# The delta rule's triangular inverse on 32x32 array tiles for four of six levels, and the sample tokens' products 128 wide

## The reference

```
a_mat = I + strict_lower(beta * decay * (k k^T))
sol   = solve_triangular(a_mat, [beta*v | beta*exp(gamma)*k])   # unit lower
w = u - wk @ S ;  o = qg @ S + (q k^T * decay) @ w ;  S = g_last*S + kd^T w
```

## Time and profile before

| | us |
|---|---|
| median of 3 runs (lowest, highest) | 2129.26 (2129.2, 2131.8) |
| the profiled execution: its time | 2131.32 |
| its span, first to last instruction | 2129.6 |
| TensorE busy | 2109.6 (99%) |
| VectorE busy | 1212.0 (57%) |
| ScalarE busy | 778.5 (37%) |
| GpSimd busy | 183.5 (9%) |
| mean granted TensorE clock | 0.996 of full speed |

### The profile page before, as it was taken

How to read it: one execution, slowest core, us unless ns; L and a number is a source line. 1 busy time by engine, 2 the same in 40 slices (tenths; PEclk the granted TensorE clock), 3 DMA queues, 4 the chain that set the end, 5 groups by cost and what they waited for, 6 DMA issues and landing times.

```text
span 2129.6 us, 34124 instructions
## 1 busy us (share of the span) xinstructions
PE 2109.6 (99%) x14525; PEld 2073.3 (97%) x14525; DVE 1212.0 (57%) x1978; ACT 778.5 (37%) x976; POOL 183.5 (9%) x347
## 2 busy tenths in 40 slices
PE   9999999999999999999999999999999999999997
PEld 9999999999999999999999999999999999999997
DVE  7988787555576566655545454444444444444444
ACT  6434554233223223334333443333333333333333
POOL 7000011110132110110000000000000000000001
PEclk9999999999999999999999999999999999999998
DMA  7544453444543444465544444444444444444443
GB/s 233 147 140 131 143 166 110 120 130 121 159 142 107 120 130 121 139 194 152 150 149 149 149 149 150 150 150 153 150 149 149 149 150 150 152 150 151 149 149 109
DMA packets 295638, 309.40 MB, mean 145 GB/s; under 512 B 9712, under 2 KB 290416, under 8 KB 295232
## 3 DMA queue, kind: packets, MB, share of 16 engines
q1 hardware_dynamic: 291616, 291.54, 44.9%
q0 software_dynamic: 3584, 15.55, 2.5%
q10 hardware_dynamic: 288, 0.15, 0.0%
HBM read 298.83 MB, written 8.37 MB: 144 GB/s over the span
## 4 chain that ended last, share of the span: by engine, by line
PE 88%; DVE 8%; ACT 2%; issue 1%; DMA 1%; SPq 0%; DVEq 0%; ACTq 0%
PE main L1494 27%; PE main L1495 27%; PE main L1496 27%; PE aux L1616 6%; DVE scratch L926 2%; DVE lo L919 2%; DVE scratch L919 1%; DMA raw<-in_w_in 1%; DVE scratch L923 1%; ACT hi L645 0%; PE aux L1726 0%; DVE qkv L926 0%; PE aux L1601 0%; ACT scratch L673 0%; SPq L241 0%
## 5 line engine op out<-in xcount | busy, mean ns | idle before, releaser
L919 DVE TENSOR_TENSOR lo<-raw,hi 128x1024 fp32r<-128x1024 f32 x546 | 660.1, 1227 | 350.9 <-ACT hi L645 343.9
L1494 PE MATMUL main<-x_hi,hi 128*128 128x320 f32 x2688 | 841.3, 313 | 4.7 <-DVE lo L919 2.3
L1496 PE MATMUL main<-x_hi,lo 128*128 128x320 f32 x2688 | 831.2, 309 | 0.0
L1495 PE MATMUL main<-x_lo,hi 128*128 128x320 f32 x2688 | 831.1, 309 | 0.0
L645 ACT ACTIVATE hi<-raw 128x1024 fp32r<-128x1024 f32 x546 | 567.3, 1054 | 696.7 <-DMA raw<-in_w_up 201.7
L1494 PEld LDWEIGHTS main<-x_hi,hi 128*128 128x128 f32 x2688 | 505.5, 188 | 12.1 <-DVE lo L919 7.4
L1495 PEld LDWEIGHTS main<-x_lo,hi 128*128 128x128 f32 x2688 | 505.6, 188 | 0.8
L1496 PEld LDWEIGHTS main<-x_hi,lo 128*128 128x128 f32 x2688 | 505.2, 188 | 0.0
L1494 PE MATMUL main<-o_hi,hi 128*128 128x320 f32 x1408 | 441.3, 313 | 0.0
L1496 PE MATMUL main<-o_hi,lo 128*128 128x320 f32 x1408 | 435.0, 309 | 0.0
L1495 PE MATMUL main<-o_lo,hi 128*128 128x320 f32 x1408 | 435.0, 309 | 0.0
(11 more groups left out here) (272 smaller groups left out, 1200.8 us busy)
## 6 DMA issues: line engine op xcount, KB each, us to landing
raw<-in_w_in SPq DMA_DIRECT2D x210, 512.0 KB, 3.6
raw<-in_w_up SPq DMA_DIRECT2D x128, 512.0 KB, 3.7
raw<-in_w_down SPq DMA_DIRECT2D x128, 512.0 KB, 3.5
raw<-in_w_back SPq DMA_DIRECT2D x80, 512.0 KB, 3.5
scratch<-in_s_in POOLq DMA_DIRECT2D x8, 512.0 KB, 4.8
out_s_out<-scratch POOLq DMA_DIRECT2D x8, 512.0 KB, 4.4
merged<-in_x SPq DMA_DIRECT2D x8, 320.0 KB, 7.7
qkv<-in_x POOLq DMA_DIRECT2D x1, 2560.0 KB, 11.2
```

Of the source, the lines that this page charges most:

```text
L919: return dve.tensor_tensor(out, a, b, op)
L1494: pe.matmul(bank, hi, xh, start=first, stop=False)
L1495: pe.matmul(bank, hi, xl, start=False, stop=False)
L1496: return pe.matmul(bank, lo, xh, start=False, stop=last)
```

## The change

The three units' 32x32 diagonal blocks are kept beside each other in compact tiles (`XTC`, `XXC`, `YYC`, 32 columns for each unit), and the first four levels (blocks up to 32) work on 32x32 tiles of the array: tile (i, i) holds the i-th diagonal block. TensorE computes Y and then (X Y)^T only; X is turned out of X^T by DVE's 32x32 transposes. At the end of level 3 (for the samples, level 1) DVE writes the blocks back to the diagonals of the full `XT` and `XX`, which POOL has cleared. TensorE's and DVE's step 2 goes. The samples' operands are read 128 columns wide: k k^T and q k^T are one product, and no product of steps 1 to 15 has a 64-column stationary operand. The wait for `tok_scaled` moves from step 4 to step 11. A new semaphore `x_cleared` holds TensorE's step 1. POOL folds the masks to 32 columns (`CM`) before the first `history`.

```diff
-            for level in range(2, 6): level_mask(level)
-            select(M1T[:], ...) x3
+            select(FM[:, 0:P], ...) x3
+            ch.link(pool.tensor_copy(FM[:, 5 * P:6 * P], ident[:]))
+            fm = FM.rearrange("p (m j c) -> p m j c", m=6, j=4)
+            ch.link(pool.tensor_tensor(fm[:, :, 0:2, :], fm[:, :, 0:2, :], fm[:, :, 2:4, :], ALU.add))
+            ch.link(pool.tensor_tensor(CM.rearrange("p (m c) -> p m c", m=6), fm[:, :, 0, :], fm[:, :, 1, :], ALU.add))
...
                 pool.dma_start(A["p_out"][h], S1).then_inc(ss_stored, 16)
+                if following:
+                    pool.memset(XT[:, 0:NP], 0.0)
+                    pool.memset(XX[:, 0:NP], 0.0).then_inc(x_cleared, 1)
...
 DVE, step 1
+                    tt(LT[:, 0:NP], AX[0][:, 0:NP], DTM[:, 0:NP], ALU.mult)
+                    link(tt(LT[0:NS, NP:N], AX[1][0:NS, N:N + NS], DTM[0:NS, NP:N], ALU.mult))
+                    for i in range(4):
+                        ins = tt(blocks(YYC, i), diagonal(LT, i), mask(0, i), ALU.mult)
+                    link(ins)
+                    tt(XTC[:, 0:2 * CB]..., mask(5), YYC[:, 0:2 * CB]..., ALU.subtract)
+                    link(tt(XTC[0:NS, 2 * CB:3 * CB], CM[0:NS, 5 * CB:6 * CB], YYC[0:NS, 2 * CB:3 * CB], ALU.subtract))
+                    dve.transpose(XXC[:, 0:2 * CB], XTC[:, 0:2 * CB])
+                    dve.transpose(XXC[0:NS, 2 * CB:3 * CB], XTC[0:NS, 2 * CB:3 * CB]).then_inc(x_ready, 1)
 DVE, even steps of levels 0 to 2 (samples: levels 0 and 1)
+                        ins = tt(XTC[:, 0:2 * CB], XTC[:, 0:2 * CB], AX[0][:, P:P + 2 * CB], ALU.subtract)
+                        link(ins)
+                        ins = dve.transpose(XXC[:, 0:2 * CB], XTC[:, 0:2 * CB])
 DVE, even step of level 3
+                        for i in range(4):
+                            r = slice(CB * i, CB * (i + 1))
+                            ins = tt(diagonal(XT, i, 2), XTC[r, 0:2 * CB]..., AX[0][r, P:P + 2 * CB]..., ALU.subtract)
+                        link(ins)
+                        for i in range(4):
+                            ins = dve.transpose(diagonal(XX, i, 2), diagonal(XT, i, 2))
...
 TensorE
-                elif k == 2:
-                    (transposes of XT, three products)
+            def tiles32(level):
+                for u in range(3 if level < 2 else 2):
+                    for i in range(4 if u < 2 else 2):
+                        yield (u, i, slice(CB * i, CB * (i + 1)), slice(CB * u, CB * (u + 1)),
+                               slice(u * P + CB * i, u * P + CB * (i + 1)))
 step 1
-                    for n, lo, hi in units:
-                        mm(AX[0][0:n, lo:hi], KT[:, lo:hi], KB[:, lo:hi])
-                        mm(AX[1][0:n, lo:hi], KT[:, lo:hi], QT[:, lo:hi])
+                    for lo in (0, P):
+                        mm(AX[0][:, lo:lo + P], KT[:, lo:lo + P], KB[:, lo:lo + P])
+                        mm(AX[1][:, lo:lo + P], KT[:, lo:lo + P], QT[:, lo:lo + P])
+                    mm(AX[1][:, NP:NP + P].rearrange("p (g n) -> p g n", g=2), wide_k[:, NP:NP + P], QKS)
 odd steps, even steps of levels 0 to 3
+                        for u, i, r, c, at in tiles32(level):
+                            ins = mm(AX[0][r, c], LT[r, at], XXC[r, c])
+                        for u, i, r, c, at in tiles32(level):
+                            ins = mm(AX[0][r, P + CB * u:P + CB * (u + 1)], YYC[r, c], XTC[r, c])
```

More of the change, by code:

```diff
@@ L31 @@
 CT = 32
+CB, SMALL_LEVELS = 32, 4
 C_MIX, C_MLP, C_FIN, C_CW = 0, KD, 2 * KD, 3 * KD
@@ L370, in level_mask @@
                 s = 2 << level
-                m = LM[:, level * P:(level + 1) * P]
+                m = FM[:, (level + 1) * P:(level + 2) * P] if level < SMALL_LEVELS else \
+                    LM[:, (level - SMALL_LEVELS) * P:(level - SMALL_LEVELS + 1) * P]
                 nb = P // (2 * s)
@@ L625, in dn_steps @@
             steps = {}
-            for k in range(19):
+            for k in (0, 1, *range(3, 19)):
                 pos = dn_place(k, False)[0] + 4
@@ L1207, in merge, with beside, diagonal, blocks @@
                     .then_inc(mlo_ready, 1)
-            both = ((P, slice(0, NP), True), (NS, slice(NP, N), False))
+            both = ((P, slice(0, NP)), (NS, slice(NP, N)))
+            def beside(t, i, j):
+                return t[CB * i:CB * (i + 1), 0:NP].rearrange("p (u x) -> p u x", u=2)[:, :, CB * j:CB * (j + 1)]
+            def diagonal(t, i, units=None):
+                if units == 2 or i >= 2:
+                    return beside(t, i, i)
+                tail = t[CB * i:CB * (i + 1), CB * i:CB * i + 2 * P + CB]
+                return bass.AP(tail.tensor, tail.offset, [list(tail.ap[0]), [P, 3], [1, CB]])
+            def blocks(t, i):
+                n = 3 if i < 2 else 2
+                return t[CB * i:CB * (i + 1), 0:n * CB].rearrange("p (u c) -> p u c", u=n)
+            def mask(m, i=None):
+                if i is None:
+                    return CM[:, None, m * CB:(m + 1) * CB].to_broadcast([P, 2, CB])
+                return CM[CB * i:CB * (i + 1), None, m * CB:(m + 1) * CB].to_broadcast([CB, 3 if i < 2 else 2, CB])
             def dn_step(h, k):
@@ L1255, in dn_step @@
                     dve.wait_ge(z_psum, h * 6 + (level + 1))
[L1256 to L1261, removed]
+                    if level < SMALL_LEVELS - 1:
+                        ins = tt(XTC[:, 0:2 * CB], XTC[:, 0:2 * CB], AX[0][:, P:P + 2 * CB], ALU.subtract)
+                        c = slice(2 * CB, 3 * CB)
+                        if level == 0:
+                            ins = tt(XTC[0:NS, c], XTC[0:NS, c], AX[0][0:NS, P + 2 * CB:P + 3 * CB], ALU.subtract)
+                        if level == 1:
+                            for i in range(2):
+                                r = slice(CB * i, CB * (i + 1))
+                                ins = tt(XT[r, NP + CB * i:NP + CB * (i + 1)], XTC[r, c], AX[0][r, P + 2 * CB:P + 3 * CB],
+                                         ALU.subtract)
+                        link(ins)
+                        ins = dve.transpose(XXC[:, 0:2 * CB], XTC[:, 0:2 * CB])
+                        if level == 0:
+                            ins = dve.transpose(XXC[0:NS, c], XTC[0:NS, c])
+                        ins.then_inc(x_ready, 1)
+                    elif level == SMALL_LEVELS - 1:
+                        for i in range(4):
+                            r = slice(CB * i, CB * (i + 1))
+                            ins = tt(diagonal(XT, i, 2), XTC[r, 0:2 * CB].rearrange("p (u c) -> p u c", u=2),
+                                     AX[0][r, P:P + 2 * CB].rearrange("p (u c) -> p u c", u=2), ALU.subtract)
+                        link(ins)
+                        for i in range(4):
+                            ins = dve.transpose(diagonal(XX, i, 2), diagonal(XT, i, 2))
+                        ins.then_inc(x_ready, 1)
+                    else:
+                        if level < 5:
+                            tt(XX[:, 0:NP], XX[:, 0:NP], AX[2][:, 0:NP], ALU.subtract)
+                        ins = tt(XT[:, 0:NP], XT[:, 0:NP], AX[3][:, 0:NP], ALU.subtract)
+                        ins.then_inc(x_ready, 1)
                 elif k == 16:
@@ L1646, in dn_step @@
                     pe.wait_ge(x_ready, h * 7 + (level + 1))
-                    for n, lo, hi in units[:3 if level < 2 else 2]:
-                        ins = mm(AX[1][0:n, lo:hi], LT[:, lo:hi], XX[:, lo:hi])
+                    if level < SMALL_LEVELS:
+                        for u, i, r, c, at in tiles32(level):
+                            ins = mm(AX[0][r, c], LT[r, at], XXC[r, c])
+                    else:
+                        if level == SMALL_LEVELS:
+                            pe.wait_ge(tok_scaled, h + 1)
+                        for lo in (0, P):
+                            ins = mm(AX[1][:, lo:lo + P], LT[:, lo:lo + P], XX[:, lo:lo + P])
                     ins.then_inc(y_psum, 1)
@@ L1652, in dn_step @@
                     pe.wait_ge(y_ready, h * 6 + (level + 1))
[L1653 to L1658, removed]
+                    if level < SMALL_LEVELS:
+                        for u, i, r, c, at in tiles32(level):
+                            ins = mm(AX[0][r, P + CB * u:P + CB * (u + 1)], YYC[r, c], XTC[r, c])
+                    else:
+                        for lo in (0, P):
+                            if level < 5:
+                                mm(AX[2][:, lo:lo + P], XT[:, lo:lo + P], YY[:, lo:lo + P])
+                            ins = mm(AX[3][:, lo:lo + P], YY[:, lo:lo + P], XT[:, lo:lo + P])
                     ins.then_inc(z_psum, 1)
```

82 lines of the change are left out of this document (38 added, 44 removed).

## The result

The median fell from 2129.23 us (2128.95 to 2131.8, 4 runs) to 2095.03 us (2094.36 to 2095.44, 4 runs): ratio 0.9835, 95% interval 0.9823 to 0.9848. The profiled execution's span is 2093.6 us, 36.0 less than that of before.

A forecast was written before the change was run, and what follows sets the result against it. TensorE's stream was taken as the bound: -18.6 us from its steps, -1.7 and +0.2 from waits in heads, +0.2 and +1.6 from POOL make -18.3, so the median 2129.3 becomes 2111.0 us. Range 2100 to 2126.

The forecast's parts named there:

- What bounds the kernel: TensorE's stream, busy 99% of the span: a microsecond taken out of it anywhere is a microsecond off the end.
- What is there today: Gaps that delta-rule steps 1 to 15 cost TensorE before the change, read from its timeline: 11.64 us per head.
- The round trip: TensorE going to another tile shape and back, charged 0.35 us once for every new step on small tiles.
- The price of an instruction on a small tile: Each 32x32 TensorE instruction in levels 0 to 3 was taken to cost 25 ns, with 18 and 37 ns as ends.
- The first rival: Instructions on small tiles overlap more than forecast: at 18 ns each the time would be 2103 us; chance 0.20.
- the loads' 18 ns: Pace of step 16's weight loads on 128x32 tiles in the earlier trace, used as a low price per small instruction.
- DVE's waits: TensorE's waits for DVE inside a head: 1.7 us less for six heads and 0.2 us more at step 10.
- The wait of step 5: TensorE's 0.28 us wait for DVE between steps 4 and 5 in regular heads goes: -1.7 us for six heads.
- Step 10: DVE's longest new step, with four transposes: 1.25 us, late by 0.1 us in the two peeled heads, +0.2 us in all.
- the prediction's own sign: The forecast was to count as wrong if TensorE waits for DVE's turned tiles in each head.
- POOL at the start: POOL's 2.1 us of mask folding ahead of the first history, less 0.5 slack, costs TensorE 1.6 us; bounds 0 and 2.5.
- The rival on PSUM: Four row tiles writing one PSUM bank take turns: 56 ns per small instruction, 2147 us; chance 0.08.

## Why the prediction was right in sign and wrong in size

- **What bounds the kernel: right.** TensorE's stream set the end, and the sum of the gaps' changes less the waits gives the span's change to 0.1 us.
- **What is there today: right.** The gaps of before needed no correction, and the 128-wide steps came out as charged, 1.77 for 1.79 and 1.12 for 1.12; alone they gave 5.7 us by the medians where the gaps say 5.1.
- **The round trip: right.** Charged 0.35 us, the line's fixed part is 0.335. The Trainium skill ("TensorEngine Tiling (Array Packing)", Key Properties) says that a change of tiling mode drains the array, and gives no price. The traces have the price; no run here shows that a drain is its cause.
- **The price of an instruction on a small tile: the step that failed.** The prediction had it as "I take 25 ns: the same quarter-wide columns, the same pair of loads and passes on one tile after another." It read the distance between starts in the earlier trace rows as what an instruction costs. It was the load of four busy tiles, 4 x 0.107 us over 16 instructions, and so it goes with the columns streamed: 64 columns gave 1.00 us in place of 1.22, and 32 columns give 0.030 us per instruction on the busiest tile. A small step has 4 to 6 on its busiest tile, 0.12 to 0.18 us, and was charged 0.40 to 0.50. Per head the eight small steps were charged 6.40 us and took 3.86, 20.3 us in all. The first rival named the mechanism, and then priced it by the loads' 18 ns, which was no price of a 32-column product either. With the 0.107 us that it used, which no row of before has but which the durations of 273 and 219 ns bear out, 32/128 x 0.107 is 0.027 us for an instruction on a tile, and that arithmetic was there to be done.
- **DVE's waits: one right, one missed.** The wait of step 5 went as forecast. Step 10 was charged 1.25 us and took 1.92: an operation on 32 partitions and 64 columns took 0.23 us (four subtractions in 0.91) or 0.245 (four transposes in 0.98), where an overlapped one was charged 0.13. The wait comes in all eight heads, 3.8 us where 0.2 was charged. By the prediction's own sign, TensorE waiting for DVE's turned tiles in each head, this term was wrong too. Step 18 of head 4 adds 0.6 us that was not charged.
- **POOL at the start: right in kind.** Charged 1.6 us. The wait near 54 us grew by 1.4, as forecast, but all waits of the first 60 us only by 0.8, and moving the fold gave 1.1 by the medians, within their noise.
- **The sum**: the 18.3 us forecast, 20.3 more for the tiles, 0.2 for step 1, 0.8 for the start, less 3.6 for the delta rule's waits (forecast 1.3 us less, measured 2.3 more), is 36.0; measured 36.0 between the spans.
- **The rival on PSUM.** No cost of the row tiles' one bank shows: four of them wrote AX[0] with starts 10 ns apart, and an instruction costs the same 0.030 us with four row tiles at work as with one. The rule of the Trainium skill ("TensorEngine Tiling (Array Packing)", Gotcha 1: PSUM Pressure) did not slow tiles that write different partitions of the bank. The Trainium skill's other two figures ("TensorE: Matmul & The Clock Gate", a floor of about 25 ns in Part 1, about 4 ns between tiles in Part 3) stand beside 9 to 10 ns in the changed kernel, 6 ns with eight tiles in use, and 33 ns on one tile: the measurement goes against the floor for instructions on different tiles.

## What to carry to other kernels

Read a group of packed matmuls by its busiest tile: the columns streamed there times the array's price for a column (here 0.84 ns, so 0.027 us for 32, against 0.030 measured), plus one round trip (here 0.34 us) for each visit, and not by the distance between starts of another shape. Put much on each visit, deal it out in turn and evenly over the tiles, and look next at the engine that hands the operands over, because there operations on 32 partitions cost as much as those on 128 (0.245 and 0.25 us for a transpose).

## What was not expected of the hardware

- Sixteen small instructions, four on each tile, add 0.12 us to the round trip, about what one tile needs for 4 x 32 columns at 0.84 ns (0.11 us), and a matmul's own duration of 0.191 us hides behind the next ones.
- The order can matter: the same instructions sorted by tile cost 0.01 us more where four in a row fell on a tile, and 0.12 more in the steps where six did.
- DVE turns 128x64 in 0.25 us and 32x64 in 0.24: four quarter-height transposes cost four times one of full height.
